# Keys and lane table loaded early into rooms of their own, transposed between the norm's last tiles; the gated output's weights loaded in two steps

## The chip, the cores and the metric

One core of one Trainium2 chip runs the whole step as one program. The metric is device time in microseconds (us) of one execution. Engines are called PE (matrix products), PEld (its weight loads), ACT, DVE, POOL and SP; SP mostly issues transfers, and its own issuing shows as SPq.

## The reference

Two layers over 512 prompt tokens and 8 sample tokens, width 1024, fp32. Layer 0 mixes by retention (4 heads), layer 1 by a diagonal state space model (SSM). After each mixer stands a PEER block: queries, scores against two key sets, a two-stage top 16, then gathered rows of two expert tables. What matters here:

```python
# layer 1's mixer, its last part
z = jax.nn.gelu(y.reshape(B, S, D)).astype(h.dtype)
a, gt = jnp.split(z @ w_glu, 2, axis=-1)
x = x + g1 * (a * jax.nn.sigmoid(gt))
# then, in both layers
h = modulate(rmsnorm(x, norm_g[i, 1]), sh2, sc2)
q = (h @ w_q).reshape(T, PEER_HEADS, 2, PEER_DQ // 2)
s1 = jnp.einsum('thd,hkd->thk', q[:, :, 0], key1)
s2 = jnp.einsum('thd,hkd->thk', q[:, :, 1], key2)
v1, i1 = lax.top_k(s1, 16); v2, i2 = lax.top_k(s2, 16)
# top 16 of the 256 sums, softmax, gather of u and v rows, weighted sum
```

## The kernel before

The program is written by hand for each engine: every engine has its own list of instructions in order, and semaphores tie them together. Nothing is scheduled by a planner. Tokens lie in five tiles: four of 128 prompt tokens and one of 8 sample tokens. `x` is the residual stream, `h` holds normed rows, `hT` the same transposed (as the products need it), `w` two slots of 2 MB for weights, `arena` a large room that the stages cut up anew, `ps` the eight accumulator banks.

The order of the stages is: modulation vectors, four retention heads, norm 1, PEER of layer 0, norm 2, SSM, gated output (GLU), norm 3, PEER of layer 1, final norm.

**A norm's end and a PEER block's start.** Norm tiles come one after another: DVE normalizes a tile into `h` (L1900, L1902), PE transposes it in eight pieces (`transposes`, L1576), ACT copies them to `hT` (L1362). Then `peer` on PE waits for the keys and for all of `hT`, transposes 16 pieces of keys (L1802), ACT copies them to `keyT` (L1482), and only then the query products start (L1827 for prompt tokens, L1828 for the samples; 16 groups). `keys` lies over the first two slots of `v_ring`. SP's list loads the keys (L1180, two transfers of 512 KB) behind the gate vectors (L1105, L1106), which wait until the last residual tile is summed; in layer 0 the small table `lane` (8 KB, L1183) comes right behind the keys, on the same semaphore.

**The end of the SSM.** The outputs come in four chunks c = 0 to 3. PE makes chunk c (L740, L743) with `toep`, a table that lies in `w`: chunks 0 and 1 in slot 0, chunks 2 and 3 in slot 1. ACT and DVE apply gelu (ACT L585, L593, L595; DVE L1028, L1033), and SP stores chunk c to `z_d` in DRAM (L485, L487). When all are stored, SP loads `z_d` back into `h` by token (L491, L492), PE transposes it (L1589) and makes the gated output in two column halves j = 0 and j = 1 (L1637 for samples, L767). Half 0 uses the two slots of `w`, half 1 uses `glu_late` in the arena, 2 MB each. SP issues all four 2 MB loads (L1074 and L478) right ahead of the store of chunk 3, after a wait for PE's chunk 3 (`yb_ps`).

SP's transfers share one queue.

Of the kernel before, what the change touches and what calls it, by code (L numbers as in the profile page):

```python
# [16 lines left out]
ACT = mybir.ActivationFunctionType  # L17
AX = mybir.AxisListType

D = 1024  # L20
P = 128
KC = D // P
TP = 4
NS = 8
TILES = TP + 1
# [4 lines left out]
BW = 512  # L30
HEADS, DK, DV = 4, 256, 512
PH, NK, TOPK = 8, 128, 16
# [117 lines left out]
def build(nc, x_prompt, x_sample, c_prompt, c_sample, state_ret, state_ssm_re, state_ssm_im,  # L150
# [4 lines left out]
    with ExitStack() as ctx:  # L155
# [46 lines left out]
        qz = cut(2, NS * NS)  # L202
        state = cut(2, DV)
        kt = cut(TP, DK)
        kz = cut(NS, DK)[0:NS]
        sring = cut(2, 2, DV)
# [21 lines left out]
        cut.at -= RING * D  # L228
        keys = cut(2 * PH, P)
        cut.at += RING * D - 2 * PH * P  # L230
# [209 lines left out]
        def ssm_sync(sp, load_block, columns, modulation, modulation_gate):  # L440
# [30 lines left out]
            for c in range(4):  # L471
                if c == 3:
                    sp.wait_ge(yb_ps, 4)
                    for b, col in ((0, 0), (1, D)):
                        load_block(b, columns(b, ssm_w_glu[0], col))
                    for b, col in ((0, BW), (1, D + BW)):
                        src = ssm_w_glu[0].rearrange("(c p) n -> p c n", p=P)[:, :, col:col + BW]
                        sp.dma_start(glu_late[b], src).then_inc(t_ld[b], 16)  # L478
                if c == 1:
                    sp.wait_ge(ca0_done, 1)  # L480
                    modulation(3)
                sp.wait_ge(z_done, c + 1)
                cols_z = slice(256 * c, 256 * (c + 1))
                out = yc[c % 2]
                sp.dma_start(z_d[0:PROMPT, cols_z].rearrange("(m t) n -> m t n", t=BL),  # L485
                             out[0:NB].rearrange("m t g n -> m t (g n)")).then_inc(zd_st[c % 2], 16)
                sp.dma_start(z_d[PROMPT:NTOK, cols_z], out[NB:NB + NS, 0].rearrange("m g n -> m (g n)")).then_inc(zd_st[c % 2], 16)  # L487
# [4 lines left out]
            sp.dma_start(h[0:NS, TP, :], z_d[PROMPT:NTOK]).then_inc(z_ld, 16)  # L492

# [23 lines left out]
        def ssm_act(act, squares, transposed, z_transposed):  # L517
# [96 lines left out]
            for i in range(2, TILES):  # L614
                transposed(3, i)

# [27 lines left out]
        def ssm_pe(pe, transposes, z_transposes, block_rows, sample_parts, sample_sum):  # L644
# [127 lines left out]
            transposes(3, TILES - 2)  # L772
            transposes(3, TILES - 1)
# [296 lines left out]
        def _(sp):  # L1070
# [85 lines left out]
            sp.dma_start(colss, decay_cols).then_inc(tab_ld, 16)  # L1156
            with sp.Fori(0, HEADS - 1) as head:
                head_blocks(head, False)
# [5 lines left out]
            def peer(layer):  # L1164
# [9 lines left out]

                query(0)
# [3 lines left out]
                for side, key in enumerate((peer_key1, peer_key2)):  # L1179
                    sp.dma_start(keys.rearrange("p (e s) d -> p e s d", s=2)[:, :, side],  # L1180
                                 key[layer].rearrange("e k d -> k e d")).then_inc(key_ld, 16)
                if layer == 0:
                    sp.dma_start(lane[:, :], lane_tab).then_inc(key_ld, 16)  # L1183
# [161 lines left out]
        def _(act):  # L1345
# [18 lines left out]

            def padding():

                act.activation(hT[:, :, NTOK:PADDED], spread(zeros[:, 0:PADDED - NTOK], 1, KC), ACT.Copy)
# [106 lines left out]
            transposed(1, TILES - 2)  # L1474
            transposed(1, TILES - 1)

            def peer(layer):
                k = 2 * layer + 2

                for b in range(4):  # L1480
                    act.wait_ge(key_ps, 4 * layer + b + 1)
                    act.activation(keyT[:, 4 * b:4 * b + 4], ps[:, b, :].rearrange("p (c r) -> p c r", c=4),  # L1482
                                   ACT.Copy).then_inc(key_done, 1)
# [77 lines left out]
            ssm_act(act, squares, transposed, z_transposed)  # L1561
# [3 lines left out]
        def _(pe):  # L1565
            def transposes(k, i):

                t, banks = NORM_TILES[k][i], NORM_BANKS[k]
                rows = ROWS[t]
                pe.wait_ge(h_done, TILES * TURN[k] + i + 1)  # L1570
                for half in range(2):
                    n = 2 * i + half
                    if n >= len(banks):
                        pe.wait_ge(hT_done, 2 * TILES * TURN[k] + n - len(banks) + 1)
                    for c in range(4):
                        mm = pe.transpose(ps[:, banks[n % len(banks)], c * P:c * P + rows],  # L1576
                                          h[0:rows, t, (4 * half + c) * P:(4 * half + c + 1) * P],
                                          ident[0:rows, 0:rows])
                    mm.then_inc(hT_ps, 1)

# [77 lines left out]
            def head_pe(head, last):  # L1658
# [130 lines left out]
                if last:  # L1789
                    transposes(1, TILES - 2)  # L1790
                    transposes(1, TILES - 1)
# [5 lines left out]
            def peer(layer):  # L1797
                pe.wait_ge(key_ld, 16 * (2 * (layer + 1) + 1))
                pe.wait_ge(hT_done, 2 * TILES * (TURN[2 * layer + 1] + 1))
                for b in range(4):  # L1800
                    for c in range(4):
                        mm = pe.transpose(ps[:, b, c * P:(c + 1) * P], keys[:, 4 * b + c], ident[:, :])  # L1802
                    mm.then_inc(key_ps, 1)
# [71 lines left out]
            ssm_pe(pe, transposes, z_transposes, block_rows, sample_parts, sample_sum)  # L1875
# [450 lines left out]
```

## Time and profile before

| what | us |
|---|---|
| median of 3 runs (lowest, highest) | 4443.08 (4434.67, 4445.8) |
| the profiled execution, its own time | 4442.77 |
| its span, first to last instruction | 4441.2 |
| PE busy | 3535.1 (80%) |
| DVE busy | 2413.1 (54%) |
| POOL busy | 2079.1 (47%) |
| ACT busy | 706.3 (16%) |

The span is the time between the first and the last instruction of the profiled execution; its own time is 1.57 us more. A timeline row tells start, length, engine, line, operation and shapes, and in brackets how long the engine had been idle and who ended that. A row of the chain of waits is a piece of the path that ended last.

### The profile page before, as it was taken

The page shows a single profiled execution, that of the slowest core. Times are in us where ns is not written, and L with a number is a line of the kernel's source. Part 1 is how long each engine was busy: PE and PEld are TensorE (multiplying, and loading weights), DVE is VectorE, ACT ScalarE, POOL GpSimd, SP SyncE. Part 2 cuts the span into 40 slices and gives each one's busy share as a digit, 9 for nine tenths or more (in the row PEclk, how much of TensorE's full clock was granted, in tenths as well). Part 3 has the DMA queues.
Part 4 walks back from the last instruction along what each step waited for, and adds up shares of the span by engine and source line. Part 5 has one row for each costly group of instructions (what it writes and reads, how often), then busy time and mean ns, then how long its engine had stood idle before and what let it go on. Part 6 is the DMA issues. An engine that isn't in the chain of part 4 may idle for free.

```text
span 4441.2 us, 31492 instructions
## 1 busy us (share of the span) xinstructions
PE 3535.1 (80%) x9590; PEld 1431.3 (32%) x9590; DVE 2413.1 (54%) x5836; ACT 706.3 (16%) x1698; POOL 2079.1 (47%) x2201
## 2 busy tenths in 40 slices
PE   5698989999777777776877974798677777777778
PEld 1233333334422222222322343344222222222223
DVE  3233232323876677687763247128766676877641
ACT  1111011011011111111111232111111111111112
POOL 0110101000577776777775400005777767777754
PEclk7789999999999999999999987899999999999999
DMA  9731314121899999999999724218999999999997
GB/s 304 252 134 57 127 43 142 57 95 55 311 408 409 409 409 398 400 409 401 396 407 408 275 54 87 104 34 292 402 409 409 409 398 401 409 404 392 409 399 266
DMA packets 415380, 1285.97 MB, mean 290 GB/s; under 512 B 59790, under 2 KB 83502, under 8 KB 414255
## 3 DMA queue, kind: packets, MB, share of 16 engines
q0 software_dynamic: 309312, 1126.31, 65.0%
q1 hardware_dynamic: 97416, 155.13, 11.0%
q10 hardware_dynamic: 8500, 2.70, 0.3%
q8 instruction: 72, 1.18, 0.1%
q14 instruction: 80, 0.66, 0.0%
HBM read 1255.20 MB, written 28.79 MB: 289 GB/s over the span
## 4 chain that ended last, share of the span: by engine, by line
PE 36%; POOL 20%; DMA 20%; DVE 12%; issue 8%; ACT 2%; SPq 1%; ACTq 0%; POOLq 0%; DVEq 0%
POOL arena L1295 10%; DMA arena<-in_peer_v_dram,arena 10%; POOL w L1295 10%; PE ps L1847 9%; PE ps L1678 8%; DMA w<-in_peer_u_dram,arena 7%; PE ps L1777 3%; DVE arena L2215 3%; PE ps L1827 3%; PE ps L767 2%; DVE w L2215 2%; DMA w<-in_w_ada_dram 2%; PE ps L1697 1%; PE ps L1706 1%; PE ps L659 1%
## 5 line engine op out<-in xcount | busy, mean ns | idle before, releaser
L1847 PE MATMUL ps<-arena 128*128 128x512 f32 x4096 | 2001.1, 620 | 621.3 <-DMA arena<-in_peer_v_dram,arena 533.1
L2215 DVE CUSTOM_DVE_ANT_0 w<-w,ps 128x1024 f32<-128x1024 f32 x896 | 1090.0, 1218 | 698.7 <-DMA w<-in_peer_u_dram,arena 697.0
L1847 PEld LDWEIGHTS ps<-arena 128*128 128x128 f32 x4096 | 722.6, 192 | 1875.1 <-DMA arena<-in_peer_v_dram,arena 1172.0
L1295 POOL DMA_INDIRECT arena<-in_peer_v_dram,arena x1040 | 989.0, 951 | 470.7 <-PE ps L1847 241.6
L1295 POOL DMA_INDIRECT w<-in_peer_u_dram,arena x912 | 860.4, 943 | 281.1 <-issue 245.4
L1517 ACT ACTIVATE arena<-ident,arena 128x128 f32<-128x128 f32 x1024 | 393.8, 398 | 1600.0 <-PE ps L1847 1575.3
L1678 PE MATMUL ps<-w,hT 128*128 128x512 f32 x768 | 346.0, 605 | 0.0
L1827 PE MATMUL ps<-hT,w 128*128 128x512 f32 x512 | 277.9, 635 | 1.4 <-ACT arena L1482 1.4
L1257 POOL DMA_DIRECT2D out_dram<-arena x32 | 23.3, 728 | 519.8 <-DVE arena L1984 375.7
L1295 POOL DMA_INDIRECT arena<-in_peer_u_dram,arena x128 | 124.7, 974 | 233.8 <-DVE arena L2147 133.3
L1678 PEld LDWEIGHTS ps<-w,hT 128*128 128x128 f32 x768 | 144.0, 192 | 203.9 <-issue 200.4
L1984 DVE SCALAR_TENSOR_TENSOR arena<-arena,ps 128x512 f32<-128x512 f32 x64 | 45.0, 745 | 274.5 <-PE ps L1697 248.9
L1236 POOL TENSOR_TENSOR rstd<-var,mhalf 128x1 f32<-128x1 f32 x25 | 18.5, 753 | 324.1 <-DVE var L1886 324.0
L2215 DVE CUSTOM_DVE_ANT_0 arena<-arena,ps 128x1024 f32<-128x1024 f32 x128 | 151.5, 1212 | 9.5 <-DMA arena<-in_peer_u_dram,arena 9.5
L1777 PE MATMUL ps<-w,arena 128*128 128x512 f32 (+1 forms) x320 | 146.9, 620 | 0.0
L1828 PEld LDWEIGHTS ps<-hT,w 128*128 128x128 f32 x512 | 97.9, 191 | 123.5 <-issue 123.5
L1612 PE MATMUL ps<-w,arena 128*32 128x512 f32 x384 | 67.4, 837 | 45.6 <-DMA w<-in_w_ada_dram 45.5
L1438 ACT ACTIVATE arena<-ps 128x512 f32<-128x512 f32 (+1 forms) x60 | 35.7, 595 | 425.2 <-PE ps L1678 406.4
L2063 DVE MAX8 arena<-modp 128x8 f32<-128x128 f32 (+1 forms) x160 | 34.6, 277 | 119.1 <-ACT modp L1490 119.1
L1229 POOL TENSOR_TENSOR mods<-arena 9x1024 f32<-9x1024 f32 x4 | 9.5, 2368 | 186.1 <-ACT arena L1391 185.7
L499 POOL MEMSET arena<- 64x2048 f32 x4 | 10.7, 2666 | 156.0 <-DVEq L997 155.9
L2215 DVE DVE_READ_ACCUMULATOR2_ANT arena<- 128x1 f32 x1024 | 83.5, 82 | 0.0
(302 smaller groups left out, 2916.3 us busy)
## 6 DMA issues: line engine op xcount, KB each, us to landing
w<-in_w_ada_dram SPq DMA_DIRECT2D x48, 1024.0 KB, 7.5
w<-in_ret_w_in_dram SPq DMA_DIRECT2D x24, 1024.0 KB, 7.2
out_dram<-arena POOLq DMA_DIRECT2D x36, 512.0 KB, 3.3
arena<-in_peer_v_dram,arena POOLq DMA_INDIRECT x1040, 10.8
arena<-in_state_ret_dram POOLq DMA_DIRECT2D x32, 512.0 KB, 5.0
w<-in_peer_w_q_dram SPq DMA_DIRECT2D x16, 1024.0 KB, 7.2
w<-in_peer_u_dram,arena POOLq DMA_INDIRECT x912, 11.2
w<-in_ret_w_out_dram SPq DMA_DIRECT2D x8, 1024.0 KB, 6.0
```

The costliest lines, as they stand in the source:

```text
L659: mm = pe.matmul(ps[:, t % 2, :], hT[:, c, t * P:(t + 1) * P], block_rows(b)[:, c, :], start=(c == 0), stop=(c == KC - 1))
L767: mm = pe.matmul(ps[:, 2 * (n % 2) + b, :], hT[:, c, t * P:(t + 1) * P], rows_of[b][:, c, :], start=(c == 0), stop=(c == KC - 1))
L1295: pool.indirect_dma_start(ring[:, slot, :], None, table, bass.IndirectOffsetOnAxis(ap=index, axis=0)).then_inc(landed_sem[slot], 16)
L1517: act.activation(diag[:, n % DIAGS], ident[:, :], ACT.Copy, scale=wgt[:, m % 4, s:s + 1]).then_inc(diag_done, 1)
L1612: mm = pe.matmul(ps[32 * j:32 * j + 32, 1 + n % 2, :], condT[:, c, :], block_rows(n % 2)[:, c, :], start=(c < 4), stop=(c >= 4))
L1678: mm = pe.matmul(ps[:, (TP * j + t) % 2, :], hT[:, c, t * P:(t + 1) * P], block_rows(j % 2)[:, c, :], start=(c == 0), stop=(c == KC - 1))
L1777: mm = pe.matmul(ps[0:rows, n % 4, :], oT[:, c, t * P:t * P + rows], rows_out[:, c, half * BW:(half + 1) * BW], start=(c == 0), stop=(c == 3))
L1827: pe.matmul(ps[:, n % 2, :], wq, hT[:, c, 0:TP * P], start=(c == 0), stop=(c == KC - 1))
L1828: mm = pe.matmul(ps[:, 2 + n % 2, 0:NS], wq, hT[:, c, TP * P:NTOK], start=(c == 0), stop=(c == KC - 1))
L1847: mm = pe.matmul(ps[:, bank + half, :], diag[:, n % DIAGS], v_ring[:, n % RING, half * BW:(half + 1) * BW], start=(n % NE == 0), stop=(n % ...
L1984: ins = dve.scalar_tensor_tensor(sring[:, b % 2, c], sring[:, b % 2, c], cols[:, 3:4], ps[:, 2 + c, :], ALU.mult, ALU.add)
L2215: dve.tensor_tensor_reduce(row, row, h_ps, 1.0, 0.0, ALU.mult, ALU.add, acts[:, j % 2, s:s + 1]).then_inc(u_used, 1)
```

## The change

Four edits:

- The keys get a room each: layer 0 the last two slots of `v_ring`, layer 1 the stretch `6 * D : 8 * D` of the arena. `qz` moves behind `kz`, so that the room of layer 0 is free once the last head's sample outputs are made. SP loads the keys ahead of the first query weights; in layer 0 after a wait for that point (`os_ps`), in layer 1 with no wait. The lane table is loaded with the tables of the heads.
- PE's key transposes and ACT's copies of them move from the head of `peer` to between the fourth and the fifth tile of the norm before it, with a new wait for the accumulator banks (`y_done` in layer 0, `glu_done` in layer 1).
- Half 0's weights go in two steps: slot 0 at chunk 1, once PE has made chunks 0 and 1; slot 1 at chunk 3, once all chunks are made.
- Half 1's weights (`glu_late`) are issued after the load of `z_d` into `h`.

```diff
@@ def ssm_sync @@
             for c in range(4):
-                if c == 3:
-                    sp.wait_ge(yb_ps, 4)
-                    for b, col in ((0, 0), (1, D)):
-                        load_block(b, columns(b, ssm_w_glu[0], col))
-                    for b, col in ((0, BW), (1, D + BW)):
-                        src = ssm_w_glu[0].rearrange("(c p) n -> p c n", p=P)[:, :, col:col + BW]
-                        sp.dma_start(glu_late[b], src).then_inc(t_ld[b], 16)
                 if c == 1:
                     sp.wait_ge(ca0_done, 1)
                     modulation(3)
+                if c % 2:
+                    sp.wait_ge(yb_ps, c + 1)
+                    load_block(c // 2, columns(c // 2, ssm_w_glu[0], c // 2 * D))
                 sp.wait_ge(z_done, c + 1)
...
             sp.dma_start(h[0:NS, TP, :], z_d[PROMPT:NTOK]).then_inc(z_ld, 16)
+            for b in range(2):
+                src = ssm_w_glu[0].rearrange("(c p) n -> p c n", p=P)[:, :, b * D + BW:(b + 1) * D]
+                sp.dma_start(glu_late[b], src).then_inc(t_ld[b], 16)
@@ sync, ahead of the heads @@
+            sp.dma_start(lane[:, :], lane_tab).then_inc(key_ld, 16)
@@ sync, peer @@
+                if layer == 0:
+                    sp.wait_ge(os_ps, HEADS * NS)
+                for side, key in enumerate((peer_key1, peer_key2)):
+                    sp.dma_start(keys_in[layer].rearrange("p (e s) d -> p e s d", s=2)[:, :, side],
+                                 key[layer].rearrange("e k d -> k e d")).then_inc(key_ld, 16)
                 query(0)
                 query(1)
                 modulation_gate(2 * layer + 1)
-                for side, key in enumerate((peer_key1, peer_key2)):
-                    sp.dma_start(keys.rearrange("p (e s) d -> p e s d", s=2)[:, :, side],
-                                 key[layer].rearrange("e k d -> k e d")).then_inc(key_ld, 16)
-                if layer == 0:
-                    sp.dma_start(lane[:, :], lane_tab).then_inc(key_ld, 16)
                 query(2)
@@ tensor @@
+            def key_transposes(layer):
+                pe.wait_ge(key_ld, 16 * (2 * (layer + 1) + 1))
+                for b in range(4):
+                    for c in range(4):
+                        mm = pe.transpose(ps[:, b, c * P:(c + 1) * P], keys_in[layer][:, 4 * b + c], ident[:, :])
+                    mm.then_inc(key_ps, 1)
@@ tensor, last head (and the same after the gated output, with glu_done) @@
                     transposes(1, TILES - 2)
+                    pe.wait_ge(y_done, HEADS * 2 * TILES + 1)
+                    key_transposes(0)
                     transposes(1, TILES - 1)
@@ scalar (and the same in ssm_act) @@
             transposed(1, TILES - 2)
+            keys_transposed(0)
             transposed(1, TILES - 1)
```

PE at the end of the last head, before: the fourth tile's last pieces, the fifth tile (L1576), the keys (L1802), the first query products.

```order
L1576 MATMUL ps<-ident,h 128x128 [waits hT_done,h_done]
L1576 MATMUL ps<-ident,h 128x128 x3
L1576 MATMUL ps<-ident,h 128x128 [waits hT_done]
L1576 MATMUL ps<-ident,h 128x128 x3
L1802 MATMUL ps<-ident,arena 128x128 [waits hT_done,key_ld]
L1802 MATMUL ps<-ident,arena 128x128 x15
L1827 MATMUL ps<-hT,w 128x512 [waits w_ld0,key_done]
```

The same place after the change (L1592 are the keys, L1583 the norm's tile, L1838 the queries); the end of norm 3 reads alike, with `glu_done` for `y_done`.

```order
L1592 MATMUL ps<-ident,arena 128x128 [waits key_ld,y_done]
L1592 MATMUL ps<-ident,arena 128x128 x15
L1583 MATMUL ps<-ident,h 128x128 [waits hT_done,h_done]
L1583 MATMUL ps<-ident,h 128x128 x3
L1583 MATMUL ps<-ident,h 128x128 [waits hT_done]
L1583 MATMUL ps<-ident,h 128x128 x3
L1838 MATMUL ps<-hT,w 128x512 [waits w_ld0,key_done,hT_done]
```

The 16 key transposes have moved ahead of the fifth tile's eight, and no longer wait for `hT`.

SP's list at the end of the SSM, before: store of chunk 2, all four weight loads, store of chunk 3, load of `z_d`, query weights.

```order
L485 DMA z_d<-h 512x1x256 [waits z_done]
L487 DMA z_d<-h 8x256
L1074 DMA w<-in_ssm_w_glu_dram 128x4x512 [waits yb_ps]
L1074 DMA w<-in_ssm_w_glu_dram 128x4x512 x3
L478 DMA arena<-in_ssm_w_glu_dram 128x8x512 x2
L485 DMA z_d<-h 512x1x256 [waits z_done]
L487 DMA z_d<-h 8x256
L491 DMA h<-z_d 128x4x1024 [waits so_st,zd_st1,zd_st0]
L492 DMA h<-z_d 8x1024
L1074 DMA w<-in_peer_w_q_dram 128x4x512 [waits glu_ps]
```

After, from the store of chunk 2 on (L481 and L483 store, L487 and L488 load `z_d`, L491 is `glu_late`, L1182 the keys); the load of slot 0 has gone ahead of the store of chunk 1.

```order
L481 DMA z_d<-h 512x1x256 [waits z_done]
L483 DMA z_d<-h 8x256
L1077 DMA w<-in_ssm_w_glu_dram 128x4x512 [waits yb_ps]
L1077 DMA w<-in_ssm_w_glu_dram 128x4x512
L481 DMA z_d<-h 512x1x256 [waits z_done]
L483 DMA z_d<-h 8x256
L487 DMA h<-z_d 128x4x1024 [waits so_st,zd_st1,zd_st0]
L488 DMA h<-z_d 8x1024
L491 DMA arena<-in_ssm_w_glu_dram 128x8x512 x2
L1182 DMA arena<-in_peer_key_dram 128x8x128 x2
```

Of the 8 MB that stood ahead of the last store, 2 MB stay there, 2 MB have moved two stores up, and 4 MB have moved behind the load of `z_d`, with the keys.

## Rows read from the trace of the kernel before

**Rows 1.** Two gather stretches: length, PE busy, PE clock, DMA share, GB/s.

```profile
1250.00:2450.00 1200.00, 922.06 (x1977) 0.98 1.02 405
3150.00:4340.00 1190.00, 913.88 (x1954) 0.98 1.02 403
```

**Rows 2.** Chain of waits, end of the SSM: start us, us, what.

```profile
2762.88 1.18 SPq L1074
...
2774.10 5.32 SPq L485
...
2779.47 10.43 DMA z_d<-h
...
2790.36 7.60 DMA h<-z_d
...
2798.16 5.22 PE ps L1589 x24
```

**Rows 3.** Timeline of DVE at the last chunk.

```profile
2768.10 2.29 DVE L1033 SCALAR_TENSOR_TENSOR h<-hT,h 72x2048 f32<-72x2048 f32 x1 [1.98 <-ACT hT L595]
```

**Rows 4.** Stretches of SP's queue: length, PE clock, DMA share, GB/s.

```profile
2744.50:2753.00 8.50, 1.00 0.00 1
2754.00:2757.00 3.00, 1.00 0.79 180
2766.00:2789.00 23.00, 0.50 1.04 384
```

**Rows 5.** Timeline of ACT and SP's issuing, chunks 1 to 3.

```profile
2734.43 2.02 ACT L585 ACTIVATE h<-ps 72x512 f32<-72x512 f32 x4
...
2740.18 0.35 SPq L1097 DMA_DIRECT2D mods<-mod_d  x1
...
2753.10 0.54 SPq L485 DMA_DIRECT2D z_d<-h  x1
...
2759.32 2.02 ACT L585 ACTIVATE h<-ps 72x512 f32<-72x512 f32 x4
```

**Rows 6.** Chain of waits, start of layer 0's PEER block.

```profile
1040.28 8.05 DMA lane<-in_lane_tab_dram
...
1048.38 3.69 PE ps L1802 x16
...
1052.74 1.12 PE ps L1827 x2
```

**Rows 7.** Timeline of PE there: the norm's last two tiles.

```profile
1040.15 1.97 PE L1576 MATMUL ps<-ident,h 128*128 128x128 f32 x8 [4.68 <-DVE h L1902]
1043.42 1.97 PE L1576 MATMUL ps<-ident,h 128*128 128x128 f32 x8 [1.30 <-DVE h L1902]
```

**Rows 8.** Stretches of PE: length, busy, granted clock, DMA share, GB/s.

```profile
1048.30:1052.00 3.70, 3.62 (x16) 0.50 0.02 4
...
2798.00:2803.00 5.00, 4.84 (x23) 0.50 0.00 0
2803.20:2804.80 1.60, 1.60 (x18) 1.00 0.00 0
...
2945.00:2949.80 4.80, 4.71 (x9) 0.50 0.00 0
```

**Rows 9.** Timeline of PE, start of layer 1's PEER block.

```profile
2934.74 1.97 PE L1576 MATMUL ps<-ident,h 128*128 128x128 f32 x8 [5.50 <-DVE h L1902]
2938.01 1.97 PE L1576 MATMUL ps<-ident,h 128*128 128x128 f32 x8 [1.30 <-DVE h L1902]
2940.76 3.65 PE L1802 MATMUL ps<-ident,arena 128*128 128x128 f32 x16 [0.78 <-ACT hT L1362]
2945.09 2.07 PE L1827 MATMUL ps<-hT,w 128*128 128x512 f32 x2 [0.69 <-ACT arena L1482]
```

**Rows 10.** Timeline of PE: the last sample output of head 3.

```profile
943.49 1.88 PE L1706 MATMUL ps<-arena 128*8 128x512 f32 x4
```

**Rows 11.** Timeline of PE: the start of the gated output's half 1.

```profile
2865.92 3.64 PE L1637 MATMUL ps<-arena,hT 128*32 128x512 f32 x32
```

More of the change, by code:

```diff
@@ L201, in build @@
         oT = cut(4, NTOK)
-        qz = cut(2, NS * NS)
         state = cut(2, DV)
@@ L205, in build @@
         kz = cut(NS, DK)[0:NS]
+        qz = cut(2, NS * NS)
         sring = cut(2, 2, DV)
@@ L227, in build @@
         v_ring = cut(RING, D)
-        cut.at -= RING * D
-        keys = cut(2 * PH, P)
-        cut.at += RING * D - 2 * PH * P
+        keys_in = [v_ring[:, RING - 2:RING, :], arena[:, 6 * D:8 * D]]
+        keys_in = [v.rearrange("p r n -> p (r n)") if len(v.shape) == 3 else v for v in keys_in]
+        keys_in = [v.rearrange("p (e d) -> p e d", d=P) for v in keys_in]
         keyT = cut(2 * PH, P)
@@ L515, in c_transposed, with ssm_act @@
                                    scale=1.0 if b < 2 else -1.0).then_inc(cT_done2, 1)
-        def ssm_act(act, squares, transposed, z_transposed):
+        def ssm_act(act, squares, transposed, z_transposed, keys_transposed):
             for n, (b, t) in enumerate(SSM_ORDER):
@@ L613, in ssm_act @@
             squares(3, TILES - 1)
-            for i in range(2, TILES):
+            for i in range(2, TILES - 1):
                 transposed(3, i)
+            keys_transposed(1)
+            transposed(3, TILES - 1)
         def c_transposes(pe):
@@ L642, in kernel_products, with ssm_pe @@
             mm.then_inc(k_ps, 1)
-        def ssm_pe(pe, transposes, z_transposes, block_rows, sample_parts, sample_sum):
+        def ssm_pe(pe, transposes, z_transposes, key_transposes, block_rows, sample_parts, sample_sum):
             def inputs(n):
@@ L772, in ssm_pe @@
             transposes(3, TILES - 2)
+            pe.wait_ge(glu_done, 2 * TILES)
+            key_transposes(1)
             transposes(3, TILES - 1)
@@ L1363, in transposed, with keys_transposed @@
                        .then_inc(hT_done, 1)
+            def keys_transposed(layer):
+                for b in range(4):
+                    act.wait_ge(key_ps, 4 * layer + b + 1)
+                    act.activation(keyT[:, 4 * b:4 * b + 4], ps[:, b, :].rearrange("p (c r) -> p c r", c=4),
+                                   ACT.Copy).then_inc(key_done, 1)
             def padding():
@@ L1478, in peer @@
                 k = 2 * layer + 2
[L1480 to L1483, printed above, removed]
                 def scores_in(p):
@@ L1560, in _ @@
             peer(0)
-            ssm_act(act, squares, transposed, z_transposed)
+            ssm_act(act, squares, transposed, z_transposed, keys_transposed)
             peer(1)
@@ L1579, in transposes @@
                     mm.then_inc(hT_ps, 1)
+            def key_transposes(layer):
+                pe.wait_ge(key_ld, 16 * (2 * (layer + 1) + 1))
+                for b in range(4):
+                    for c in range(4):
+                        mm = pe.transpose(ps[:, b, c * P:(c + 1) * P], keys_in[layer][:, 4 * b + c], ident[:, :])
+                    mm.then_inc(key_ps, 1)
             def z_transposes():
@@ L1797, in peer @@
             def peer(layer):
-                pe.wait_ge(key_ld, 16 * (2 * (layer + 1) + 1))
                 pe.wait_ge(hT_done, 2 * TILES * (TURN[2 * layer + 1] + 1))
[L1800 to L1803, printed above, removed]
                 def score_of(p, i):
@@ L1874, in _ @@
             peer(0)
-            ssm_pe(pe, transposes, z_transposes, block_rows, sample_parts, sample_sum)
+            ssm_pe(pe, transposes, z_transposes, key_transposes, block_rows, sample_parts, sample_sum)
             peer(1)
```

## The prediction, on record before the result

> **What bounds the kernel now.** I read the page first, then the chain of waits, then timelines and stretches around the three places that the change touches. Two thirds of the time lie in the gather stretches of the two PEER blocks, where the transfers run at 405 and 403 GB/s with the DMA engines full [rows 1]. The change doesn't touch them; they start when the queries are made, so whatever is won ahead of a block moves it forward as a whole. Ahead of the blocks the work is a chain, and the chain of waits shows three holes in it.
>
> The first is at the end of the SSM. DVE is done with the last chunk at 2768.10 + 2.29 = 2770.4 [rows 3], but the store of it is issued at 2774.10, takes 5.32 us to issue and lands 10.43 us after 2779.47, at 2789.9 [rows 2]: the queue is full from 2766 to 2789 at 384 GB/s [rows 4] with 8 MB of weights issued ahead of it from 2762.88 on [rows 2]. Then `z_d` comes back (issued from about 2790.0, landed 7.60 us after 2790.36) and PE starts at 2798.16 [rows 2]. PE sits idle through all of that, and nothing else is on the path.
>
> The second and third are at the start of each PEER block. In layer 0 PE has transposed the last norm tile by 1043.42 + 1.97 = 1045.4 [rows 7], waits until 1048.38 for keys and lane table, and then does 3.69 us of key transposes; the queries start at 1052.74 [rows 6]. In layer 1 the keys are there in time, but the same work, 3.65 us from 2940.76, and a last copy stand ahead of the queries at 2945.09 [rows 9]. In both places PE had waited for the norm just before: 4.68 us and 1.30 us in layer 0 [rows 7], 5.50 us and 1.30 us in layer 1 [rows 9].
>
> **Part 1: the weights and the last store.** Slot 0's 2 MB is issued when SP is done with the modulation rows, 2740.18 + 0.35 = 2740.5; its new wait, PE's chunk 1, is over by then, since ACT copies that chunk out at 2734.43 [rows 5]. Behind this wait stand SP's later stores, and for them ACT. The queue carries 1 GB/s from 2744.5 to 2753.0 [rows 4]; 2 MB at 384 GB/s is 5.5 us, so it is through by about 2750, ahead of the store of chunk 1 at 2753.10 [rows 5]. Were that cover gone, ACT would feel it only past 2759.32, where it writes over that store's rows [rows 5]; bytes of the store are done by 2757 [rows 4]. I cost it at nothing, at most 2 us.
>
> Slot 1's 2 MB stays where it was: issued from 2762.88, moving from about 2766 (the store of chunk 2 is ahead of it), through at 2766 + 5.5 = 2771.5. The last store, issued at 2770.4, then meets a queue that is free as it gets there. The store of chunk 1 shows what one takes on a free queue: issued 2753.10, bytes to 2757, 3.9 us [rows 4, 5]. So bytes end near 2774.3, and with the 0.7 us between the end of bytes (about 2789.2) and the landing (2789.9) that the old one shows, `z_d` is complete at 2775.0 in place of 2789.9. From there to PE it was 2798.16 - 2789.9 = 8.26 us [rows 2]; now 4 MB of `glu_late` and 1 MB of keys are queued behind, not ahead. If the queue serves in order, PE starts at 2783.2: **15.0 us** gained. If the load shares the engines with what is behind it, all 6.3 MB of `z_d` and `glu_late` land together: 16.4 us at 384 GB/s plus some 1.9 us of start and landing from 2775.0, PE at 2793.3, gain 4.9 us. I take 15.0: the old order itself shows service in turn, since the store issued last, a mere 0.5 MB, landed only when the 8 MB were through [rows 2, 4]. `glu_late` is needed at 2865.92 [rows 11], now 2851; it and the keys are there by 2795 even at the slow end, so 55 us of products hide them.
>
> **Part 2: keys in layer 0.** The loads: SP's new wait ends with the last sample output, 943.49 + 1.88 = 945.4 [rows 10]; behind it stand only loads for the block, the first of which waited for later products anyway. The keys have 95 us until PE wants them; lane comes with the tables at the start, 8 KB. Both cost nothing. On PE the sequence becomes: fourth tile at 1040.15 (1.97 us), keys 3.69, fifth tile 1.97 (its `h` was ready at 1043.42) [rows 6, 7]: 7.63 us with no gap, if the clock stays low. All these rows are at a granted clock of 0.50, the lower level of 1.2 GHz. Now the clock matters: in the run of `z_d` transposes from 2798.16 it stood at 0.50 up to 2803.0 and at 1.00 from 2803.2 [rows 2, 8], 4.9 us after a start from idle; the key transposes at 1048.3 stayed at 0.50 for their first 3.7 us [rows 8]. A run of 7.63 us is longer than either, so I expect the rise 4.9 us in; the remaining 2.7 us shrink to 1.4, and PE is done 6.3 us after 1040.15. From PE's last transpose to the next PE work is 0.8 us (2939.98 to 2940.76) [rows 9]. The queries start at 1040.15 + 7.1 = 1047.2 in place of 1052.74, at full clock as before: **5.5 us**.
>
> **Part 3: keys in layer 1.** The same sequence from 2934.74 [rows 9] (all shifted by part 1): queries at 2941.8 in place of 2945.09, 3.3 us. And before, they ran at 0.50 until 2949.8, 4.8 us [rows 8] at half speed, 2.4 us lost; now they should start at 1.00. Together **5.7 us**.
>
> For both, a bound from below: the clock doesn't rise before the queries. Then the queries start after 7.63 + 0.8 = 8.4 us, gains of 4.2 and 1.9 us, and layer 0 pays 2.4 us for a slow start that it didn't have: 1.8 + 1.9 = 3.7 us in place of 11.2. From above: a rise after 3.7 us gives 0.6 us more for each.
>
> One rule of the Trainium skill speaks against the 11.2. "TensorE: Matmul & The Clock Gate", section "Part 4: PE-mode transpose", says that transposes don't count as work for the clock's rise. By that rule parts 2 and 3 would bring the 3.7. The trace disagrees: the rise at 2803 came while nothing but transposes had run [rows 2, 8].
>
> ACT's copies of the keys (0.60 us each, one for four transposes of 0.9 us) go beside PE. The new waits on `y_done` and `glu_done` are over before the fourth tile is normed, since DVE's order has the last product read ahead of that.
>
> **The sum.** 15.0 + 5.5 + 5.7 = 26.2 us, against the profiled execution's own 4442.77: 4416.6. The median of the runs stands 0.3 us above that execution; forecast 4417 us, -0.6%.
>
> **The rivals.**
> - *The transposes don't lift the clock.* For it: the two key runs in the trace ended at 0.50 or as it rose. Against it: the `z_d` run [rows 8]. Gain 15.0 + 3.7 = 18.7, time 4424.
> - *The load of `z_d` shares the queue's engines with the 4 MB behind it.* For it: 16 engines each run on to the next transfer as they finish. Against it: the old store's landing. Gain 4.9 + 11.2 = 16.1, time 4427.
> - *The change doesn't bring the last store forward*, because slot 1's load still stands in its way and is slower than 384 GB/s, the store waiting for the last of it. At half the rate it costs 5.5 us of the 15.0: 4422.
> - *Slower.* The gather stretches, some 2400 us at 405 and 403 GB/s [rows 1], run at a lower rate because a block starts with its eight-slot ring in another step with DVE and PE. The two stretches differ by 0.5%, 6 us each, for no visible reason. To eat 26 us they would both have to lose 1.1%; from 1.7% on (40 us, 4457) it is slower than before. That is three times the spread seen.
>
> **How the numbers follow.** Chances: forecast 0.62 (4412 to 4422), clock 0.12, shared queue 0.13, store held up 0.06, slower gathers 0.04; 0.03 for a gain that is larger still (an earlier rise in both blocks and a quicker `z_d`: 4410). The three runs of before spread by 11 us, so a median may sit 3 to 4 us off; 4409 to 4428 then leaves under 2 in 10 out. The bound of 0.3%, about what a measurement of this kernel can tell from no change, is 13.3 us, a time of 4429.8: all but the slower case and a part of the shared queue's lie below it. Faster 0.88, same 0.09, slower 0.03.
>
> **What would show it.** In the profile after: the last store of `z_d` issued right behind DVE's last piece, in under 1 us, and PE's transposes of `z_d` some 13 us after DVE's last piece in place of 27.8 (part 1); if it is 20 or more, the queue is shared. Eight, sixteen and eight transposes in one run at each norm's end, the clock at 1.00 before the run is out, and queries some 7 us after the fourth tile's start (12.6 and 10.4 before). The slots' and keys' loads must land with nobody waiting. It is wrong if gather stretches grow, or if ACT or DVE wait at chunk 3 for the store of chunk 1.

## The result and the profile after

The changed kernel takes **4416.37 us** (median of 4 runs, 4414.6 to 4417.88); the kernel before took 4444.44 us beside it. The ratio is 0.9941, with a 95% interval from 0.9924 to 0.9958, so a gain of 19 to 34 us. The forecast was 4417. The profiled execution took 4417.88 us with a span of 4416.3 us; before, the span was 4441.2 us. The span is 24.9 us shorter.

The chain of waits of the changed kernel, at the end of the SSM (start us, us, what), answers to [rows 2]:

```profile
2764.89 2.30 DVE h L1036
2767.21 0.52 SPq L481
2767.77 3.76 DMA z_d<-h
2771.59 0.37 SPq L487
2772.00 7.70 DMA h<-z_d
2779.89 2.81 PE ps L1603 x12
```

The last store follows DVE's last piece (ended 2767.19) at once, is issued in 0.52 us (5.32 before) and lands 3.76 us later (10.43 before). The load of `z_d` takes 7.70 us (7.60 before), now with 5 MB issued behind it. From DVE's last piece to PE it is 12.7 us, where it was 27.8.

What SP issued there, in the changed kernel's timeline of SP:

```profile
2737.01 1.54 SPq L1077 DMA_DIRECT2D w<-in_ssm_w_glu_dram  x2
2749.88 0.56 SPq L481 DMA_DIRECT2D z_d<-h  x1
...
2759.67 2.24 SPq L1077 DMA_DIRECT2D w<-in_ssm_w_glu_dram  x2
...
2772.45 3.37 SPq L491 DMA_DIRECT2D arena<-in_ssm_w_glu_dram  x2
2775.86 10.61 SPq L1182 DMA_DIRECT2D arena<-in_peer_key_dram  x2
```

And the stretches of its queue, as in [rows 4] (length, PE clock, DMA share, GB/s):

```profile
2742.00:2748.00 6.00, 1.00 0.88 319
...
2759.50:2768.30 8.80, 0.50 0.94 293
2768.40:2771.00 2.60, 0.50 0.90 217
2773.00:2794.20 21.20, 0.77 0.99 345
```

Slot 0's 2 MB (2742 to 2748) are through ahead of the store of chunk 1 (2749.88), and slot 1's are through by 2768.3, just as the last store's bytes start. The key loads block SP for 10.61 us while the queue is full, and nobody waits for SP then. `glu_late` and keys are there by 2794.

PE's timeline of the changed kernel at the end of the two norms, layer 0 and then layer 1, answers to [rows 6, 7, 9]:

```profile
1040.45 1.97 PE L1583 MATMUL ps<-ident,h 128*128 128x128 f32 x8 [4.68 <-DVE h L1913]
1042.21 3.49 PE L1592 MATMUL ps<-ident,arena 128*128 128x128 f32 x16
1045.54 1.04 PE L1583 MATMUL ps<-ident,h 128*128 128x128 f32 x8
1047.37 1.12 PE L1838 MATMUL ps<-hT,w 128*128 128x512 f32 x2 [0.79 <-ACT hT L1366]
...
2915.60 1.97 PE L1583 MATMUL ps<-ident,h 128*128 128x128 f32 x8 [5.50 <-DVE h L1913]
2917.36 2.89 PE L1592 MATMUL ps<-ident,arena 128*128 128x128 f32 x16
...
2921.97 1.12 PE L1838 MATMUL ps<-hT,w 128*128 128x512 f32 x2 [0.84 <-ACT hT L1366]
```

Stretches of PE in the same kernel (length, busy, granted clock, DMA share, GB/s), as in [rows 1, 8]:

```profile
1040.50:1045.30 4.80, 4.80 (x23) 0.50 0.62 231
1045.80:1048.80 3.00, 2.21 (x13) 1.00 0.03 5
...
1250.00:2450.00 1200.00, 921.34 (x1971) 0.98 1.02 405
...
2537.20:2540.40 3.20, 3.20 (x8) 0.50 1.02 352
...
2915.60:2919.10 3.50, 3.50 (x17) 0.50 0.00 0
...
3135.00:4325.00 1190.00, 917.78 (x1961) 0.98 1.02 402
```

In both layers the last two tiles and the keys are one run of transposes. It starts at the clock's lower level (0.50, 1.2 GHz) and ends at the upper one, so the second tile of norm takes 1.04 us where the first takes 1.97, and the queries run at 1.00. The gather stretches run at 405 and 402 GB/s, as before (405 and 403).

The span by stretches, from the rows above and those of before, in order of time:

| stretch | before us | after us | difference |
|---|---|---|---|
| start to layer 0's 4th tile | 1040.15 | 1040.45 | +0.3 |
| 4th tile to first query, layer 0 | 12.59 | 6.92 | -5.7 |
| first query to DVE's last chunk of the SSM | 1717.65 | 1719.81 | +2.2 |
| DVE's last chunk to `z_d` transposes | 27.77 | 12.71 | -15.1 |
| `z_d` transposes to layer 1's 4th tile | 136.58 | 135.71 | -0.9 |
| 4th tile to first query, layer 1 | 10.35 | 6.37 | -4.0 |
| first query, layer 1, to the end | 1496.1 | 1494.3 | -1.8 |

They add up to -24.9 (to rounding). The last line holds what the queries of layer 1 used to lose at 0.50 [rows 8]: their fourth group started 5.60 us after the first before and 3.27 us after the change, 2.3 us less.

### The profile page after: what moved, and what is told of

The parts are those of the page before. It is cut to its first block, busy times and chain, and to the rows that moved or that the text cites. A ratio compares the mean times of both kernels' runs of the same rounds, so it can differ in the third digit from the quotient of the medians.

```text
span 4416.3 us, 31492 instructions
## 1 busy us (share of the span) xinstructions
PE 3530.7 (80%) x9590; PEld 1431.5 (32%) x9590; DVE 2411.8 (55%) x5836; ACT 706.0 (16%) x1698; POOL 2080.0 (47%) x2201
## 4 chain that ended last, share of the span: by engine, by line
PE 34%; DMA 21%; POOL 21%; DVE 12%; issue 8%; ACT 2%; SPq 1%; ACTq 0%; POOLq 0%; DVEq 0%
POOL arena L1299 10%; POOL w L1299 10%; DMA w<-in_peer_u_dram,arena 10%; DMA arena<-in_peer_v_dram,arena 9%; PE ps L1692 8%; PE ps L1858 7%; PE ps L1791 3%; DVE arena L2226 3%; PE ps L1838 3%; PE ps L768 3%; DVE w L2226 2%; DMA w<-in_w_ada_dram 2%; PE ps L1711 1%; PE ps L1720 1%; PE ps L660 1%
## 5 line engine op out<-in xcount | busy, mean ns | idle before, releaser
L1838 PE MATMUL ps<-hT,w 128*128 128x512 f32 x512 | 275.7, 631 | 1.6 <-ACT hT L1366 1.6
```

The lines of the kernel that those rows point to most:

```text
L1838: pe.matmul(ps[:, n % 2, :], wq, hT[:, c, 0:TP * P], start=(c == 0), stop=(c == KC - 1))
```

## The experiments

The theory was the prediction's: three separate gains that add, the queue served in the order of issue, and a run of transposes that lifts the clock by itself. The rivals: a queue whose transfers share the engines; a gain in the layers that is due to the early loads alone; and the order of the loads at the SSM's end being immaterial.

One finding of all profiles has to come first. The start of layer 0's fourth tile lies ahead of all that most of these kernels change, and yet it came anywhere between 1031 and 1043 us in the twelve profiles. Whole times of single executions scatter by several us for a reason outside of the touched places. So the experiments are read by intervals inside a profile, with the medians beside them: **S2**, from the end of DVE's last chunk to the `z_d` transposes; **S1** and **S4**, from the fourth tile's start to the first query in layers 0 and 1.

| kernel | median us | ratio, 95% interval | S2 | S1 | S4 | queries at 0.50 for (layer 0, 1) |
|---|---|---|---|---|---|---|
| before | 4444.44 | | 27.77 | 12.59 | 10.35 | 0, 4.8 us |
| after | 4416.37 | 0.9924 to 0.9958 | 12.71 | 6.92 | 6.37 | 0, 0 |
| weights only | 4423.96 | 0.9953 to 0.9981 | 12.87 | 12.84 | 10.36 | 4.7, 4.1 us |
| keys only | 4426.86 | 0.9959 to 0.9984 | 29.29 | 6.92 | 6.69 | 0, 0 |
| late ahead of the store | 4419.81 | 0.9942 to 0.9967 | 22.69 | 6.92 | 6.68 | 0, 0 |
| late behind the store | 4422.98 | 0.9948 to 0.9973 | 22.36 | 6.92 | 6.52 | 0, 0 |
| both slots at chunk 3 | 4417.60 | 0.9929 to 0.9957 | 17.19 | 6.93 | 6.93 | 0, 0 |
| keys behind the 5th tile | 4424.99 | 0.9950 to 0.9976 | 12.64 | 10.29 | 10.29 | 3.9, 3.8 us |
| keys ahead of the 4th tile | 4418.90 | 0.9938 to 0.9965 | 12.92 | 5.92 | 5.92 | 4.7, 6.4 us |
| the same, keys twice, filled wait | 4415.82 | 0.9929 to 0.9956 | 12.80 | 5.41 | 5.53 | 5.3, 5.0 us |
| after, filled | 4407.73 | 0.9918 to 0.9947 | 12.97 | 5.10 | 5.10 | 0, 0 |
| after, again | 4415.56 | 0.9924 to 0.9957 | 13.49 | 6.92 | 6.39 | 0, 0 |

The kernel before, beside the experiments, took 4440.11 (first four), 4440.45 (next four) and 4441.58 us (last two). That is 3 to 4 us less than beside the changed kernel, and a part of what the foretold whole times miss by.

**The parts alone.** First, the kernel before with only the loads at the SSM's end changed:

```diff
-                if c == 3:
-                    sp.wait_ge(yb_ps, 4)
-                    for b, col in ((0, 0), (1, D)):
-                        load_block(b, columns(b, ssm_w_glu[0], col))
-                    for b, col in ((0, BW), (1, D + BW)):
...
-                        sp.dma_start(glu_late[b], src).then_inc(t_ld[b], 16)
...
+                if c % 2:
+                    sp.wait_ge(yb_ps, c + 1)
+                    load_block(c // 2, columns(c // 2, ssm_w_glu[0], c // 2 * D))
...
             sp.dma_start(h[0:NS, TP, :], z_d[PROMPT:NTOK]).then_inc(z_ld, 16)
+            for b in range(2):
...
+                sp.dma_start(glu_late[b], src).then_inc(t_ld[b], 16)
```

> The kernel before with part 1 alone: slot 0's weights at chunk 1, slot 1's at chunk 3, the 4 MB of half 1 behind the load of z_d; keys and lane table as before. Theory (each part moves its own hole in the chain, and the gather stretches only follow): 15 us faster than before, about 4429 us; from DVE's last chunk to PE's transposes of z_d 12.7 us as in the changed kernel, in place of 27.8; the starts of both PEER blocks as in the kernel before. Rival (the parts overlap, or part 1 alone moves a wait to the norm behind it): under 10 us.

Then the rest alone, which is the changed kernel with these lines put back:

> The changed kernel with part 1 undone: the four weight loads ahead of the last store again; keys and lane early and transposed between the norm's tiles. Theory (chain and clock): about 11 us faster than before, 4433 us: 5.5 us in layer 0, and in layer 1 3.3 to 4 us of chain plus some 2.4 us because the queries start at a clock of 1.00. Rival (the chain alone counts, the clock is as low at the queries' start as it was): 4.2 + 1.9 = 6 us or less, 4438 us, with the first queries of both blocks at 0.50.

The chain of waits at the SSM's end, weights only (start us, us, what):

```profile
2766.81 0.52 SPq L481
2767.37 3.67 DMA z_d<-h
...
2771.51 7.95 DMA h<-z_d
```

The same chain with the keys only:

```profile
2773.33 5.50 SPq L485
2778.87 10.49 DMA z_d<-h
2789.82 8.03 DMA h<-z_d
```

Each part keeps its own interval: the loads give S2 (12.87) and leave S1 and S4 as they were; the keys give S1 and S4 and leave S2 long, at 29.29 (1.5 more than before; S2 of one and the same order of loads isn't the same in every execution). The medians lie 16 and 13 us under before (15 and 11 foretold). Together that is 29, against 28 and 26 us for the whole in its two comparisons. The parts add, as far as these intervals can tell. The price of each is better read from the intervals, since in the weights-only kernel layer 0's queries ran at 0.50 for 4.7 us though nothing there was edited. That missed the expectation that this block would start as in the kernel before, and it shows that the unedited block can lose half of that, 2.35 us, which it didn't lose in the profile of before.

**Where `glu_late` stands in the queue.** The 4 MB are moved from behind the load of `z_d`, once to a place ahead of the last store and once between the store and the load:

```diff
                     load_block(c // 2, columns(c // 2, ssm_w_glu[0], c // 2 * D))
+                if c == 3:
+                    for b in range(2):
...
+                        sp.dma_start(glu_late[b], src).then_inc(t_ld[b], 16)
...
             sp.dma_start(h[0:NS, TP, :], z_d[PROMPT:NTOK]).then_inc(z_ld, 16)
-            for b in range(2):
...
-                sp.dma_start(glu_late[b], src).then_inc(t_ld[b], 16)
```

> The changed kernel, but the 4 MB of half 1 are issued ahead of the last store again, right behind slot 1's load. Theory (every megabyte ahead of the store delays it, in order): 4.2 million bytes at 384 GB/s are 10.9 us, so DVE's last chunk to PE's transposes of z_d becomes 12.7 + 10.9 = 23.6 us and the time 4427 us. Rival (the two-step load of the slots is what frees the store, the 4 MB lie beside it): 12.7 us stay, 4416 us.

```diff
+            for b in range(2):
...
+                sp.dma_start(glu_late[b], src).then_inc(t_ld[b], 16)
             sp.wait_ge(zd_st[0], 64)
...
             sp.dma_start(h[0:NS, TP, :], z_d[PROMPT:NTOK]).then_inc(z_ld, 16)
-            for b in range(2):
...
-                sp.dma_start(glu_late[b], src).then_inc(t_ld[b], 16)
```

> The changed kernel, but the 4 MB of half 1 are issued behind the last store and ahead of the load of z_d (which waits for the store to land). Theory (the queue serves in order): the load's bytes wait until the 4 MB are through, about 8 us later than in the changed kernel: 20.8 us from DVE's last chunk to PE, time 4424 us. Rival (the engines share out what is queued): both loads move at once, the load of z_d is done about 4.6 us later, 17.3 us, time 4421 us, and then the 4 MB behind it in the changed kernel must have cost it something too.

The chain of waits with `glu_late` ahead of the store:

```profile
2759.59 3.66 SPq L485
2763.30 10.65 DMA z_d<-h
2774.41 7.66 DMA h<-z_d
```

And with `glu_late` behind the store:

```profile
2766.47 3.85 DMA z_d<-h
2770.37 2.93 SPq L490
2773.34 14.70 DMA h<-z_d
```

Wherever the 4 MB stand, the transfer issued right behind them pays: the store lands in 10.65 us in place of 3.76, or the load in 14.70 in place of 7.70, and the one ahead of them pays nothing (the load 7.66, the store 3.85). That is a queue served in turn. S2 grows by 10.0 and 9.7 us, where 10.9 and 8 us were foretold. The second was foretold too short by 1.6 us; 8 us is what comes out if the 4 MB run from their issue on. But while the store was on its way (2766.4 to 2770.4) the queue moved 204 GB/s, 0.8 MB, of which the store is 0.5 MB; so nearly all of the 4 MB still stood ahead of the load. The medians, 4419.81 and 4422.98 us, lie below the foretold 4427 and 4424 us; the first is only 3.4 us above the changed kernel, and its profiled execution had won 6.7 us ahead of layer 0's fourth tile (1033.74 in place of 1040.45), where nothing differs.

**Whether slot 0 had to come early.** Both slots are loaded at chunk 3, `glu_late` stays behind the load of `z_d`:

```diff
-                if c % 2:
-                    sp.wait_ge(yb_ps, c + 1)
-                    load_block(c // 2, columns(c // 2, ssm_w_glu[0], c // 2 * D))
+                if c == 3:
+                    sp.wait_ge(yb_ps, 4)
+                    for b in range(2):
+                        load_block(b, columns(b, ssm_w_glu[0], b * D))
```

> The changed kernel, but both slots are loaded at chunk 3, as before; the 4 MB of half 1 stay behind the load of z_d. Theory (in order): 2.1 million bytes more ahead of the last store, 5.5 us: 18.2 us from DVE's last chunk to PE's transposes of z_d, time 4422 us. Rival (slot 0's early load collides with the stores of chunks 1 and 2 in the changed kernel, so the two steps bring nothing): 12.7 us, 4416 us.

The chain of waits of that kernel:

```profile
2769.76 8.17 DMA z_d<-h
2778.39 7.79 DMA h<-z_d
```

The last store lands in 8.17 us in place of 3.76, so the second step is worth 4.5 us and the way of `glu_late` to the back of the queue some 10: of the 15 us of part 1, two thirds come from `glu_late`. S2 was foretold at 18.2 us and measured 17.19. The median (4417.60 us; 4422 foretold) doesn't separate this kernel from the changed one.

**Where the key transposes stand.** The early loads are kept in both kernels. In one the transposes stand behind the norm's fifth tile, as before; in the other ahead of the fourth (here layer 0; layer 1 likewise, and ACT's copies in step):

```diff
                     transposes(1, TILES - 2)
-                    pe.wait_ge(y_done, HEADS * 2 * TILES + 1)
-                    key_transposes(0)
                     transposes(1, TILES - 1)
...
                 pe.wait_ge(hT_done, 2 * TILES * (TURN[2 * layer + 1] + 1))
+                key_transposes(layer)
```

> The changed kernel, but the key transposes and their copies stand at the head of each PEER block again, behind the fifth tile; keys and lane are loaded early all the same. Theory (chain and clock): layer 0 loses the wait for keys and lane (2.3 to 3.0 us) and no more, layer 1 loses nothing, and the clock rises as late as in the kernel before or later: queries start 10.3 to 10.4 us after the fourth tile's start in both layers, in place of 6.9 and 6.4, and layer 1's (perhaps layer 0's too) begin at 0.50. Time 4416 plus 3.4 plus 4.0 plus 2 to 5 for the clock: 4426 us. Rival (early loads are the gain, the place of the transposes is not): 4417 us.

```diff
-                    transposes(1, TILES - 2)
                     pe.wait_ge(y_done, HEADS * 2 * TILES + 1)
                     key_transposes(0)
+                    transposes(1, TILES - 2)
                     transposes(1, TILES - 1)
```

> The changed kernel, but the key transposes stand ahead of the fourth tile, in the idle time of PE before it, in place of between the fourth and the fifth. Rival (the chain alone counts): the fifth tile follows its own norm, the queries start 6.0 us after the fourth tile's start in place of 6.9 (layer 0) and 6.4 (layer 1), 1.3 us faster, 4415 us. Theory (the run of 32 transposes without a gap is what lifts the clock): with the keys out of it the two tiles leave a gap, the queries start 6.0 us after the fourth tile but at 0.50 for 3 to 6 us in each block, which costs 1.5 to 3 us each: 4418 to 4421 us, slower than the changed kernel in spite of the shorter chain.

PE's timeline in layer 0, first with the keys behind the fifth tile:

```profile
1032.53 1.60 PE L1580 MATMUL ps<-ident,h 128*128 128x128 f32 x8 [4.68 <-DVE h L1909]
1035.80 1.97 PE L1580 MATMUL ps<-ident,h 128*128 128x128 f32 x8 [1.67 <-DVE h L1909]
1038.45 3.67 PE L1589 MATMUL ps<-ident,arena 128*128 128x128 f32 x16 [0.69 <-ACT hT L1363]
1042.82 2.07 PE L1834 MATMUL ps<-hT,w 128*128 128x512 f32 x2 [0.69 <-ACT arena L1369]
```

And with the keys ahead of the fourth:

```profile
1031.06 1.60 PE L1583 MATMUL ps<-ident,h 128*128 128x128 f32 x8 [2.80 <-DVE h L1913]
1034.33 1.97 PE L1583 MATMUL ps<-ident,h 128*128 128x128 f32 x8 [1.67 <-DVE h L1913]
1036.98 2.07 PE L1838 MATMUL ps<-hT,w 128*128 128x512 f32 x2 [0.69 <-ACT hT L1366]
```

The queries (2.07 us for two products, where the changed kernel has 1.12) tell the clock at once. Counting half of the time at 0.50 as lost, the queries start in effect 12.2 us after the fourth tile in both layers with the keys behind, against 12.6 and 12.75 before. What the early loads bring by themselves isn't fixed by that: in the weights-only kernel the same unedited block of layer 0 comes to 12.84 + 2.35 = 15.2 us, so in layer 0 it lies between 0.4 and 3 us, depending on where the clock happened to rise; in layer 1, where the keys were in time anyway, the half microsecond lies in the clock alone. But in layer 0 keys and lane table landed at 1048.3 before [rows 6], and between the tiles the key transposes start at 1042.2: there the early loads are what makes that place possible. With the keys ahead of the tile it is 8.3 and 9.1 us, although the first query comes 1.0 us (layer 0) and 0.5 us (layer 1) sooner than in the changed kernel; there it is 6.9 and 6.4. So between the tiles is the best of the three places by these intervals (whole times alone don't separate the three, the intervals of their ratios overlap): there the keys fill the gap and, with the tiles, make one run out of which the clock rises. With the keys ahead of the fourth tile the clock fell to 0.50 at 1031.5, inside that tile, in layer 0, and at 2908.8, in the gap behind it, in layer 1; the fifth tile, with idling of 1.67 us (2.18 in layer 1) ahead of it, didn't bring it back.

**Could the clock be held up?** First the last kernel with all keys transposed twice (the first pass for nothing), and 125 transposes of the identity in the wait for `z_d`:

```diff
+            pe.wait_ge(yb_done, 12)
+            for n in range(125):
+                pe.transpose(ps[:, 0, 0:P], ident[:, :], ident[:, :])
             pe.wait_ge(yb_done, 16)
...
                 for b in range(4):
+                    for c in range(4):
+                        pe.transpose(ps[:, b, c * P:(c + 1) * P], keys_in[layer][:, 4 * b + c], ident[:, :])
+                for b in range(4):
```

> As the kernel with the keys ahead of the fourth tile, but the 16 key transposes are made twice, to keep PE at work while it waits for the norm, and 125 transposes of the identity fill PE's wait for z_d. Their results are not used. Theory (transposes count for the clock): the clock stays at 1.00 through both tiles and the queries start at 1.00 some 5 us after the fourth tile's start (tile 1.0 us, copy 0.8 us behind the fifth tile's norm), 1.3 to 1.9 us earlier than in the changed kernel in each block; the transposes of z_d take 4 to 5 us in place of 5.7. About 4412 us, 4 us faster than the changed kernel. Rival (transposes don't count): clock at 0.50 as without the filling, queries slow at their start, 4418 us or more.

PE's timeline: the fifth tile of layer 0, then the filled wait:

```profile
1038.45 1.46 PE L1586 MATMUL ps<-ident,h 128*128 128x128 f32 x8 [2.17 <-DVE h L1919]
...
2747.32 13.81 PE L749 MATMUL ps<-ident 128*128 128x128 f32 x125
2773.52 5.67 PE L1609 MATMUL ps<-ident,h 128*128 128x128 f32 x40 [12.39 <-DVEq L1050]
```

Stretches there (length, PE busy, clock, DMA share, GB/s):

```profile
2747.40:2761.00 13.60, 13.60 (x126) 1.00 0.57 176
...
2766.40:2773.40 7.00, 0.00 (x0) 0.50 0.97 347
```

This missed in both places. In the layers the fourth tile did run at 1.00, but behind the gap that follows it the clock fell, half a microsecond into the fifth tile (at 1039.0 and 2913.0), and the queries ran at 0.50 for 5 us. At `z_d` the filling ran at once, was over 12.4 us too early, and the transposes that it was for took 5.67 us, as in the changed kernel (5.70). What it does show: with nothing but transposes PE stood at 1.00 for 13.6 us, and idle PE was at 0.50 before `z_d` came.

The other kernel keeps the changed order, puts 36 identity transposes ahead of the fourth tile and 225 into the wait for `z_d`:

```diff
+            pe.wait_ge(yb_done, 12)
+            for n in range(225):
+                pe.transpose(ps[:, 0, 0:P], ident[:, :], ident[:, :])
             pe.wait_ge(yb_done, 16)
...
-                    transposes(1, TILES - 2)
                     pe.wait_ge(y_done, HEADS * 2 * TILES + 1)
+                    for n in range(36):
+                        pe.transpose(ps[:, 0, 0:P], ident[:, :], ident[:, :])
+                    transposes(1, TILES - 2)
                     key_transposes(0)
```

> The changed kernel in its own order, with transposes of the identity in PE's idle time: 36 ahead of the fourth tile of each norm (0.11 us each at a clock of 1.00, 4.0 us of the 4.7 and 5.0 us that PE waits there) and 225 in the wait for z_d (24.8 us). Their results are not used. Theory (transposes hold the clock up): it stands at 1.00 through tile, keys and tile, so the fourth tile takes 1.0 us and the keys 1.9 us, the fifth tile follows its own norm, and the queries start at 1.00 some 5.1 to 5.4 us after the fourth tile's start, in place of 6.9 and 6.4; from the transposes of z_d to the first products of the gated output 5 us in place of 6.2. About 4 us below the changed kernel, too little for the timed runs to tell. Rival (transposes don't count): the clock falls as before, all three stretches stay as they are or the queries start at 0.50.

PE's timeline of it:

```profile
1031.72 4.15 PE L1811 MATMUL ps<-ident 128*128 128x128 f32 x36
1036.49 1.09 PE L1588 MATMUL ps<-ident,h 128*128 128x128 f32 x8 [0.62 <-DVE h L1920]
...
1041.59 1.12 PE L1845 MATMUL ps<-hT,w 128*128 128x512 f32 x2 [0.74 <-ACT hT L1371]
...
2746.86 24.73 PE L749 MATMUL ps<-ident 128*128 128x128 f32 x225
2771.81 4.27 PE L1608 MATMUL ps<-ident,h 128*128 128x128 f32 x40 [0.23 <-DVEq L1052]
```

And a stretch (columns as above):

```profile
2747.00:2771.60 24.60, 24.58 (x226) 1.00 0.71 236
```

Here the clock stands at 1.00 all the way in all three places. S1 and S4 fall to 5.10 us, 1.8 and 1.3 less than in the changed kernel, and from the start of the `z_d` transposes to the first product of the gated output it is 5.17 us in place of 6.19: 4.1 us by the intervals (4.2 against the second profile of the changed kernel). Its median, 4407.73 us (4405.82 to 4413.22), is the lowest of all, 8 us under the changed kernel run again beside it. But the intervals of the two ratios overlap, and so do the single runs, so the whole time alone doesn't show a gain over the changed kernel; what is shown is the 4.1 us inside the profiles.

**The changed kernel again**, beside the last one:

> The changed kernel itself once more, beside the filled one on the same chip. Theory: 6.4 to 7.4 us from the fourth tile to the queries in both blocks, queries at 1.00 from their start, 12.7 us from DVE's last chunk to the transposes of z_d, some 26 us below the kernel before. Rival (the clock's rise inside the run of transposes was luck of that one execution): queries that start at 0.50 in one block or both.

It repeats S1 and S4 to 0.02 us (6.92 and 6.39) with the queries at 1.00, so the rise inside the run was not luck of one execution. S2 is 13.49 us, 0.8 more than foretold, and the median 4415.56 us, with single runs from 4403.78 to 4421.36.

## Why the prediction was right, step by step

- **Part 1, the store: right; that it is right to 0.1 us is luck.** Forecast 15.0, measured 15.06 (27.77 to 12.71). Over the seven profiles with this order of loads S2 lies between 12.64 and 13.49, and the old order gave 27.77 and 29.29. The cover held: slot 0 was through some 2 us ahead of the store of chunk 1. The step that the prediction had to choose, a queue served in turn, is shown by the load's 7.70 us with 5 MB behind it, and by the two kernels that move `glu_late`. The rival of the shared queue (4427) is out. So is the one in which slot 1 holds the store up (4422): its load was through by 2768.3, 1.1 us after the store's issue, and the store landed as fast as the sum had it.
- **Part 2, layer 0: right in mechanism, and in size against this profile of before.** Forecast 5.5, measured 5.67. The clock was to rise 4.9 us into the run; it rose at 1045.4, 5.0 us in. The run is some 0.4 us shorter than the sum's 7.63 us at 0.50, which adds up row lengths: the keys start 1.76 us after a tile of 1.97. S1 after the change is 6.92 or 6.93 us in six profiles, but the block as it was costs 12.6 us in the profile of before and 15.2 in that of weights only, so the gain in layer 0 is 5.7 to 8.3 us. The prediction put no separate price on the early loads.
- **Part 3, layer 1: right in mechanism, a term mis-sized.** Forecast 3.3 + 2.4 = 5.7, measured 3.98 + 2.3 = 6.3. The term that was off is the 4.9 us to the clock's rise, which I had taken over from the `z_d` run: here it came at 2919.4, 3.8 us in. That is near the upper bound of the text, a rise after 3.7 us, 0.6 us more. In other profiles with this order it came 3.8 to 5.0 us in (S4 6.37 to 6.93), so the term has no one size.
- **The clock.** That transposes lift it was the choice with a rival of its own (4424), and it holds: with nothing but transposes since the engine's idling, the clock rose 3.8 to 5.0 us into the unbroken runs of the layers and 2.9 to 5.9 us into those of `z_d`. A run of 3.7 us with idling of 0.69 us on either side (keys behind the fifth tile) ended at 0.50. The Trainium skill, "TensorE: Matmul & The Clock Gate", section "Part 4: PE-mode transpose", says that they don't count as work for it. For these fp32 transposes the measurement decides against that: those rises, and 24.6 us of nothing but transposes at 1.00 in the filled kernel.
- **What was not in the sum.** The parts make 27.0 us, the span lost 24.9. 1.7 us went at the end of the second norm, where the clock fell to 0.50 from 2537.2 to 2540.4 for transposes and first products; before, it stood at 1.00 there, with the same 2.04 us of idling ahead of the last tile. It fell so in six of the twelve profiles (after, after again, weights only, both kernels with `glu_late` moved, both slots at chunk 3), with and without the key edits, and no load of part 1 had been moved yet by that time. Its cause is open; it isn't tied to one of the parts. 0.9 us came back at the `z_d` transposes, where the clock rose 2.9 us in (4.9 before).
- **The slower rival** (gathers at a lower rate, 4457) is out: 405 and 402 GB/s. The "two thirds of the time" that the prediction gives to these stretches is the share of the whole PEER blocks; its rows 1 hold 2390 of 4441 us, 54%. Nothing in the sum hangs on it.
- **The total.** 26.2 forecast; 24.9 in the profiles, 28.1 and 26.0 by medians, with an interval of 19 to 34. That the total is this close owes something to small misses of either sign: part 3's 0.6 and the 0.9 at `z_d` against the 1.7 at the second norm.

## What to carry to other kernels

Where a short transfer that the path waits for shares a queue with weights, look at what was issued ahead of it: here 4 MB behind the load in place of ahead of the store were worth 10 us, and the move cost nothing, since nobody wanted the weights for another 50 us. Work that must be done anyway is best put into a gap ahead of a chain's last step, next to the engine's other work, so that it fills the wait and the clock is up when the chain goes on; its place was worth 11 us over two layers by the intervals, and in layer 0 the early loading is what made that place possible. And read an edit of a few us by intervals inside the profile, since the whole time moved by more than that for reasons elsewhere.

## What the runs showed of the hardware

Identity transposes in a wait held PE at 1.00 (2.4 GHz) for 24.6 us, while in the changed kernel, with PE idle from 2753.9, the granted clock was 0.50 from about 2759 on; filling three waits brought 4.1 us. Where the filling ended 12.4 us ahead of the work that it was for, it brought nothing. With the keys ahead of the fourth tile, in layer 0, the clock fell 0.4 us into that tile, behind 2.80 us of idling, and stayed at 0.50 through the fifth; with the keys done twice it fell half a microsecond into the fifth tile, behind 2.17 us of idling. Unbroken runs of transposes that began at 0.50 saw the clock rise after 2.9 to 5.9 us, at different points in different places and executions. The engine SP stood for 10.6 us on two issues to a full queue at no cost, because nothing was queued behind them that anybody waited for.
